# Latent attention of a two-block kernel: rotation on transposed features, softmax by groups of heads, first tile against its own keys

## The reference, cut to what matters

```python
def mla_mixer(x, cos, sin, w_in, q_norm, kv_norm, w_uq, w_ukv, w_out):
    c_q, c_kv, k_rope = jnp.split(x @ w_in, [256, 512], axis=-1)        # 256 + 256 + 64 columns
    q  = (rms_norm(c_q, q_norm) @ w_uq)    # 8 heads x (128 plain + 64 rotated)
    kv = (rms_norm(c_kv, kv_norm) @ w_ukv) # 8 heads x (128 key + 128 value)
    q_rope = rope(q_rope, cos, sin); k_rope = rope(k_rope, cos, sin)   # one rotated key for all heads
    s  = (q_nope . k_nope + q_rope . k_rope) * 192 ** -0.5
    s  = where(key_chunk <= query_chunk, s, -inf)    # chunks of 64 tokens
    return (softmax(s) @ v) @ w_out                  # w_out: 1024 x 1024
```

## Time and profile before

| | us |
|---|---|
| median of three runs | 3115.67 |
| profiled execution | 3120.56 |
| its span, first to last instruction | 3118.6 |
| PE busy | 2941.4 (94%) |
| DVE busy | 1938.2 (62%) |
| ACT busy | 1544.7 (50%) |
| mean granted TensorE clock | 0.966 of full |

### The profile page before, as it was taken

How to read it: one execution, slowest core, us unless ns; L and a number is a source line. 1 busy time by engine, 2 the same in 40 slices (tenths; PEclk the granted TensorE clock), 3 DMA queues, 4 the chain that set the end, 5 groups by cost and what they waited for, 6 DMA issues and landing times.

```text
span 3118.6 us, 38381 instructions
## 1 busy us (share of the span) xinstructions
PE 2941.4 (94%) x15294; PEld 2454.3 (79%) x15294; DVE 1938.2 (62%) x2879; ACT 1544.7 (50%) x2264; POOL 73.5 (2%) x98
## 2 busy tenths in 40 slices
PE   8999999899999999998999999985999999999999
PEld 6879878678788798776788878873788878887887
DVE  5556977665565579775655764562545764567645
ACT  5554734455455546434554644452444544464554
POOL 0000000000000000000000000000000000000000
PEclk9999998899999999998999999996999999999999
DMA  7544410355555434104554445540454655452552
GB/s 280 186 141 152 155 48 15 125 185 186 172 192 186 163 129 136 42 8 162 185 186 167 154 158 182 169 166 27 145 182 152 212 181 186 163 191 96 191 182 81
DMA packets 127650, 469.40 MB, mean 151 GB/s; under 512 B 14478, under 2 KB 14654, under 8 KB 126320
## 3 DMA queue, kind: packets, MB, share of 16 engines
q1 hardware_dynamic: 124416, 452.55, 42.6%
q0 software_dynamic: 3056, 14.39, 1.4%
HBM read 465.84 MB, written 1.05 MB: 150 GB/s over the span
## 4 chain that ended last, share of the span: by engine, by line
PE 79%; DVE 12%; ACT 5%; issue 2%; POOL 1%; DMA 0%; POOLq 0%; ACTq 0%; DVEq 0%
PE ps L589 76%; DVE w_lo_part L1920 2%; PE ps L761 2%; DVE hc L2226 1%; DVE conv_acc L2151 1%; ACT w_hi_part L1399 1%; PE ps L626 1%; ACT wx_hi_part L1399 0%; DVE wx_lo_part L1920 0%; DVE h_lo_part L1962 0%; DVE x_res L2063 0%; DVE zs L2369 0%; ACT gdn_rhs L1666 0%; POOL gdn_gate L2671 0%; DVE x_res L2121 0%
## 5 line engine op out<-in xcount | busy, mean ns | idle before, releaser
L1920 DVE TENSOR_TENSOR w_lo_part<-w_raw,w_hi_part 128x1024 fp32r<-128x1024 f32 x458 | 551.2, 1216 | 366.4 <-ACT w_hi_part L1399 365.0
L1399 ACT ACTIVATE w_hi_part<-w_raw 128x1024 fp32r<-128x1024 f32 x458 | 476.3, 1053 | 421.4 <-PE ps L589 421.3
L589 PE MATMUL ps<-w_hi_part,h_hi_part 128*128 128x512 f32 (+2 forms) x1348 | 543.2, 403 | 35.9 <-DVE w_lo_part L1917 8.6
L589 PE MATMUL ps<-w_hi_part,h_lo_part 128*128 128x512 f32 (+2 forms) x1348 | 529.6, 393 | 0.0
L589 PE MATMUL ps<-w_lo_part,h_hi_part 128*128 128x512 f32 (+2 forms) x1348 | 529.5, 393 | 0.0
L1920 DVE TENSOR_TENSOR wx_lo_part<-wx_raw,wx_hi_part 128x1024 fp32r<-128x1024 f32 x222 | 268.2, 1220 | 218.2 <-ACT wx_hi_part L1399 217.8
L1399 ACT ACTIVATE wx_hi_part<-wx_raw 128x1024 fp32r<-128x1024 f32 x222 | 231.6, 1057 | 231.4 <-PE ps L589 231.3
L589 PEld LDWEIGHTS ps<-w_hi_part,h_hi_part 128*128 128x128 f32 x1348 | 259.7, 193 | 96.6 <-issue 18.3
L589 PEld LDWEIGHTS ps<-w_hi_part,h_lo_part 128*128 128x128 f32 x1348 | 259.2, 192 | 55.2
L589 PEld LDWEIGHTS ps<-w_lo_part,h_hi_part 128*128 128x128 f32 x1348 | 260.1, 193 | 49.8
L589 PE MATMUL ps<-wx_hi_part,h_hi_part 128*128 128x512 f32 x712 | 285.7, 401 | 6.4 <-ACT lv L1729 2.1
(11 more groups left out here) (432 smaller groups left out, 4857.9 us busy)
## 6 DMA issues: line engine op xcount, KB each, us to landing
w_raw<-in_weights SPq DMA_DIRECT2D x568, 512.0 KB, 3.3
wx_raw<-in_weights SPq DMA_DIRECT2D x288, 512.0 KB, 3.3
row<-in_rows POOLq DMA_DIRECT2D x8, 1024.0 KB, 5.2
row<-in_rows POOLq DMA_DIRECT2D x8, 512.0 KB, 4.0
const<-in_const SPq DMA_DIRECT2D x1, 1088.0 KB, 16.1
x_res<-in_x SPq DMA_DIRECT2D x2, 512.0 KB, 6.5
ple_p<-in_p POOLq DMA_DIRECT2D x4, 256.0 KB, 5.1
out<-x_res SPq DMA_DIRECT2D x2, 512.0 KB, 2.6
```

Of the source, the lines that this page charges most:

```text
L589: return nc.tensor.matmul(out, lhsT, rhs_, start=start, stop=stop, skip_group_check=True)
L1399: A(hi_of(s)[:, 0:wd], raw_of(s)[:, 0:wd], ACT.Copy).then_inc(*up("w_hi", u))
L1920: V.tensor_tensor(lo_of(s)[:, 0:wd], raw_of(s)[:, 0:wd], hi[:, 0:wd], ALU.subtract).then_inc(*up("w_lo", u))
```

## The change

Only `mla` and what feeds it is changed, on all engines.

- **Head.** The norm weights are no longer columns applied after the turn but a row (`mnorm`) applied before it. Each tile has its own square root and its own turn (`turn_c`). The angles are computed with features on partitions and the 256 tokens in the free dimension.
- **Rotation.** The packing adds the rotated-query weights with the halves of each head exchanged (`mla_uq_swap`) and the rotated-key weights beside their exchanged copy (`mla_kr`). The rotation becomes product times cosine plus exchanged product times signed sine, on features, with no turn afterwards. For the key the sum is taken by PE with the identity. There is one more weight unit (857 instead of 856), and the key's unit is full width.
- **Softmax.** Heads are scored in groups: for tile 0 two groups of four heads against 128 keys, for tile 1 four groups of two heads against 256 keys. The mask is a third matmul into the last 64 keys with one contraction row (`mrow`, `mla_masked` in the trace). Maxima and exponentials read PSUM; DVE, no longer ACT, copies the turned probabilities. PE's order interleaves the groups.
- **Output.** The last product takes its input tile by tile and half by half, as the gated linear attention did.

Of `mla`'s own functions the diff shows the new lines; the lines that they replace stand in the listing above.

```diff
-            rows("mla_w_in_2", j, 0, 512, MR)
-            for c in range(0, MH, 4):
-                feature("mla_uq_nope", j, c * P, 2, 4)
-            rows("mla_uq_rope", j, 0, 0, 512)
-            for c in range(0, MH, 4):
-                feature("mla_uk", j, c * P, 2, 4)
+            feature("mla_kr", j, 0)
+            feature("mla_uq_rope", j, 0, 2, 4)
+            feature("mla_uq_swap", j, 0, 2, 4)
+            for w in ("mla_uq_nope", "mla_uk"):
+                for c in range(0, MH, 4):
+                    feature(w, j, c * P, 2, 4)
...
+        HEADS = [[[0, 2, 4, 6], [1, 3, 5, 7]], [[0, 2], [1, 3], [4, 6], [5, 7]]]
+        SCORE_BANK = [[2, 3], [6, 7, 4, 5]]
...
+                def turn_c(t):
                     pe.wait_ge(*when("mcn", (tag, t)))
                     for c in range(4):
+                        last_ = nc.tensor.transpose(ps[:, t, c * P:(c + 1) * P], mcn[:, t, c * P:(c + 1) * P], ident)
+                    last_.then_inc(*up("turned", (tag + ".c", t)))
+
+                def chunks(banks, first, key):
+                    s = next_unit()
+                    for c in range(4):
+                        out = ps[:, banks[c // 2], (c % 2) * SEQ:(c % 2 + 1) * SEQ]
+                        last_ = feature_chunk(s, out, mc_hi[:, first:first + 2], mc_lo[:, first:first + 2], 2, c * 2)
+                    last_.then_inc(*up("w_used", key))
+
+                def score(t, g):
+                    tok, nk = slice(t * P, (t + 1) * P), (t + 1) * P
+                    for n, h in enumerate(HEADS[t][g]):
+                        o = ps[:, SCORE_BANK[t][g], n * nk:(n + 1) * nk]
+                        b = (h % 2) * MR
+                        mm(o, mqnT[:, h, tok], mknT[:, h, 0:nk], True, False)
+                        mm(o, mqrT[b:b + MR, h // 2, tok], mkrT[b:b + MR, 0:nk], False, False)
+                        last_ = mm(o[:, nk - CH:], mrow[0:1, 0:P], mrow[0:1, P:], False, True)
+                    last_.then_inc(*up("mscore", (tag, t, g)))
+
+                def turn_p(t, g):
+                    pe.wait_ge(*when("mexp", (tag, t, g)))
+                    if t and g >= 2:
+                        pe.wait_ge(*when("mpT_out", (tag, t, g - 2)))
+                    elif t:
+                        pe.wait_ge(*when("mpT_out", (tag, 0, g)))
+                    for n, h in enumerate(HEADS[t][g]):
+                        for k in range(t + 1):
+                            at = (n * (t + 1) + k) * P
+                            last_ = nc.tensor.transpose(ps[:, g % 2, at:at + P], msc[t][:, slot_of(h), k * P:(k + 1) * P], ident)
+                    last_.then_inc(*up("mpT", (tag, t, g)))
+
+                def output(t, b):
+                    pe.wait_ge(*when("mpT_out", (tag, t, 2 * b + 1 if t else 1)))
+                    for h in range(4 * b, 4 * b + 4):
+                        for k in range(t + 1):
+                            last_ = mm(ps[:, (6 if t else 2) + b, (h % 4) * P:(h % 4 + 1) * P], mpT[t][:, slot_of(h), k, :],
+                                       mv[:, k, h * P:(h + 1) * P], k == 0, k == t)
+                    last_.then_inc(*up("mo", (tag, t, b)))
+
+                turn_c(0)
+                s = next_unit()
+                feature_chunk(s, ps[:, 6, 0:SEQ], h_hi, h_lo, KC).then_inc(*up("w_used", ("mkr", tag)))
+                turn_c(1)
+                pe.wait_ge(*when("mkr_parts", tag))
+                for n in range(2):
+                    o = ps[n * MR:(n + 1) * MR, 3, 0:SEQ]
+                    mm(o, ident[:, 0:MR], mkr[:, :], True, False)
+                    last_ = mm(o, ident[:, MR:], mkr[:, :], False, True)
+                last_.then_inc(*up("mkr_sum", tag))
+                for t in range(NT):
+                    pe.wait_ge(*when("h_lo", (tag + ".c", t)))
+                chunks([6, 7], 0, ("mqr", (tag, 0)))
+                chunks([0, 1], 0, ("mqr", (tag, 1)))
                 pe.wait_ge(*when("mkr_out", tag))
+                chunks([2, 3], 0, ("mqn", (tag, 0)))
+                chunks([4, 5], 0, ("mqn", (tag, 1)))
+                pe.wait_ge(*when("roped", (tag, 0)))
+                chunks([6, 7], 2, ("mkn", (tag, 0)))
+                pe.wait_ge(*when("roped", (tag, 1)))
+                chunks([0, 1], 2, ("mkn", (tag, 1)))
+                slots = [next_unit(), next_unit()]
+                for t in range(NT):
+                    pe.wait_ge(*when("mT", (tag, "q", t)))
+                    for k in range(2):
+                        last_ = row_chunk(slots[k], lambda t, n: ps[:, 2 + 2 * t + n, :], mc_hi[:, 2 + k, :], mc_lo[:, 2 + k, :],
+                                          0, k == 0, k == 1, tiles=[t])
+                        if t:
+                            last_.then_inc(*up("w_used", *([("product", tag + ".v")] if k else [])))
+                    if t == 0:
+                        last_.then_inc(*up("mv_first", tag))
+
+                pe.wait_ge(*when("roped", (tag, 2)))
+                pe.wait_ge(*when("mT", (tag, "k", 1)))
+                pe.wait_ge(*when("mrow", tag))
+                pe.wait_ge(*when("evacuated", (tag + ".v", 0)))
+                score(0, 0)
+                score(0, 1)
+                score(1, 0)
+                turn_p(0, 0)
+                score(1, 1)
+                turn_p(0, 1)
                 pe.wait_ge(*when("evacuated", (tag + ".v", 1)))
+                score(1, 2)
+                output(0, 0)
+                output(0, 1)
+                score(1, 3)
+                turn_p(1, 0)
+                turn_p(1, 1)
+                output(1, 0)
+                turn_p(1, 2)
+                turn_p(1, 3)
+                output(1, 1)
...
+                def exps(t, g):
+                    nk = (t + 1) * P
+                    act.wait_ge(*when("mmax", (tag, t, g)))
+                    for n, h in enumerate(HEADS[t][g]):
+                        p = slot_of(h)
+                        A(msc[t][:, p, :], ps[:, SCORE_BANK[t][g], n * nk:(n + 1) * nk], ACT.Exp, scale=MLA_SCALE,
+                          bias=mst[:, 1, t, p:p + 1], accum_out=mst[:, 2, t, p:p + 1]).then_inc(*up("mexp", (tag, t, g)))
+
+                square(0)
                 act.wait_ge(*when("angle", tag))
+                A(rope[:, :, :], red[:, :, :], ACT.Sin).then_inc(*up("sine", tag))
+                take_c(0)
+                square(1)
+                weights(4)
+                take_c(1)
                 weights(1)
+                act.wait_ge(*when("mkr_sum", tag))
+                A(mkrT[:, :], ps[:, 3, 0:SEQ], ACT.Copy).then_inc(*up("mkr_out", tag))
                 weights(2)
+                copied(mqnT, 2, "q", 0)
+                weights(1)
+                copied(mqnT, 4, "q", 1)
+                weights(1)
+                copied(mknT, 6, "k", 0)
+                weights(1)
+                copied(mknT, 0, "k", 1)
+                weights(1)
+                act.wait_ge(*when("mv_first", tag))
+                A(mv[:, 0, :], acc(2, 0), ACT.Copy).then_inc(*up("evacuated", (tag + ".v", 0)))
                 act.wait_ge(*when("w_used", ("product", tag + ".v")))
+                A(mv[:, 1, :], acc(2, 1), ACT.Copy).then_inc(*up("evacuated", (tag + ".v", 1)))
+                exps(0, 0)
+                exps(0, 1)
+                for g in range(4):
+                    exps(1, g)
+                weights(2)
...
                 dve.wait_ge(*when("mla_in", tag))
+                link(V.tensor_copy(angle[:, :], posi[:, :]))
+                link(V.tensor_scalar(angle[:, :], angle[:, :], invf[:, 0:1], None, ALU.mult))
                 for n, shift in enumerate((0.0, 0.25)):
+                    link(V.tensor_scalar(turns[:, n, :], angle[:, :], 1.0 / TWO_PI, shift, ALU.mult, ALU.add))
+                link(V.tensor_scalar(turns[:, :, :], turns[:, :, :], ROUND, None, ALU.add))
+                link(V.tensor_scalar(turns[:, :, :], turns[:, :, :], ROUND, None, ALU.subtract))
+                link(V.scalar_tensor_tensor(red[:, :, :], turns[:, :, :], -PI_PARTS[0], over(angle[:, :], 2), ALU.mult, ALU.add))
+                for part in PI_PARTS[1:]:
+                    link(V.scalar_tensor_tensor(red[:, :, :], turns[:, :, :], -part, red[:, :, :], ALU.mult, ALU.add))
+                link(V.tensor_scalar(red[:, 1, :], red[:, 1, :], 0.25 * TWO_PI, None, ALU.add))
+                V.tensor_scalar(red[:, :, :], red[:, :, :], PI_IN, -PI_IN, ALU.min, ALU.max).then_inc(*up("angle", tag))
+                link(V.memset(mrow[0:1, 0:P], 0.0))
+                link(V.memset(mrow[0:1, 0:CH], 1.0))
+                V.memset(mrow[0:1, P:], -1e30).then_inc(*up("mrow", tag))
+                mean(0)
+                normed_c(0)
+                take_c(0)
+                mean(1)
+                normed_c(1)
                 weights(4)
+                dve.wait_ge(*when("sine", tag))
+                dve.wait_ge(*when("w_used", ("mkr", tag)))
+                for n in range(2):
+                    r = slice(n * MR, (n + 1) * MR)
```

(36 more changed lines are left out.)

293 lines of the change are left out of this document (93 added, 200 removed).

## The result

The kernel after takes 3076.3 us (median of 4, 3074.6 to 3078.22), the kernel before 3119.69 in the runs beside it. The ratio is 0.9859 with a 95% interval of 0.9842 to 0.9876, so 39 to 49 us less, 44 in the middle. The forecast was 48 less, from 3115.67 to 3068. The measured 3076.3 is 8.3 above that figure and outside the 3062 to 3073 that the prediction gave 0.58, though inside its wider 3059 to 3082; 4.0 of it is that the kernel before took 3119.69 here and not 3115.67. Between the two profiled executions the spans differ by 42.2 us (3118.6 to 3076.4).

The account below looks back on a forecast made before the run. It took PE's stream of matmuls, 79% of the chain, as the bound. Head +4.9, projections +1.4, rotation -14.7 and attention -39.6 sum to -48.0 us, from 3115.67 to 3068; range 3062 to 3073 (0.58), wider 3059 to 3082.

Parts of the forecast that it names:

- Piece 3: Rotation, between projections and scores: small instructions, wait, turns and copies go, 14.7 us becomes 0.
- Piece 2: Projections, first up-projection to their end: 23.0 us becomes 24.4, 1.4 us more, half-clock start included.
- Piece 1: Head, latent product to first up-projection: starts 4.9 us later, bounds +2 to +9.
- four float32 matmuls of 256 columns, 1.15 us each: In the head, PE's adding of the rotated key's parts at half clock: 4.6 us.
- Piece 4: Attention, first score to first output matmul: 74.2 us becomes 34.6, 39.6 us less.
- A float32 matmul of 128 columns is 0.26, the mask 0.23.: Full-clock score prices in the attention, giving tile 0 6.0 us and PE's work there 27.0 us.
- Scores keep the clock.: In the attention, scores hold PEclk at 1.00 but don't raise it; 1.5 us added for drops at the end waits.
- the prediction's own sign: Stated test in the attention: the prediction is wrong if PEclk reads 0.50 during tile 1's scores.
- My first rival: Any gap in tile 1's scores drops PEclk to 0.50, costing 8.5 us: 3075; cases at 3074 to 3076 together 0.22.
- the head didn't become the bound: Rival: the head's serial chain takes its upper end and masks cost 0.4: 3075; cases at 3074 to 3076 together 0.22.
- Columns are saved: Rival denied: 128-column score matmuls cost as much as 256, tile 0 8 x 0.74 more: 3074; cases 3074 to 3076 together 0.22.
- The slow case: Rival: PE stays at half clock through attention, output projection and first MLP, 3119 us; not faster or slower 0.04.

Follow-up runs that it names:

- e10: Kernel before with rotary products contracting over 128 rows, using two zeroed key copies: 3104.6 us against 3120.51, ratio 0.9946.
- e2: Kernel after with the rotary product contracting over all 128 rows and the mask matmuls left out: 3050.86 us, ratio 0.9791 against the kernel before.
- e5: Kernel after with every score matmul, rotary and mask, zero-padded to 128 rows and nothing left out: 3054.92 us, ratio 0.9791 against the kernel before.
- e3: Kernel after with the 16 mask matmuls left out, all else unchanged: 3058.26 us, ratio 0.9815 against the kernel before.
- e6: Kernel after with only the mask matmul filled up to 128 rows; rotary product keeps 64: 3062.16 us, ratio 0.9817 against the kernel before.
- e7: Kernel after with only the rotary product filled up to 128 rows; mask keeps one row: 3060.48 us, ratio 0.9809 against the kernel before.
- e11: e7 with each one-row mask matmul issued three times: 3082.8 us, ratio 0.9876 against the kernel before.
- e4: Kernel after with the rotary key's product moved ahead of the first latent turn: 3075.46 us, ratio 0.9869 against the kernel before.

## Why the prediction came near, step by step

**Piece 3 was right.** PE goes from the values to the scores without a wait.

**Piece 2 was right**, 24.2 for 24.4, the slow start included.

**Piece 1 was right in its mechanism and mis-sized in one term.** Both waits stand where they were forecast. The term "four float32 matmuls of 256 columns, 1.15 us each" took 1.9 us for 4.6. Two things were wrong in it. The 1.15 came from the stretch whose row counts alternate; without that a matmul costs 0.85 at half clock (e10, 2121.99 to 2122.84). And the four fill two halves of the array's columns; their weight loads stand in pairs in the trace (2084.11, 2084.60, 2085.02), and they took about the time of two: 2 x 0.85 = 1.7. That is 2.7 of the 3.3 us; the rest, 0.6, are the angles. The root came as forecast.

**Piece 4 is the step that failed: "74.2 becomes 34.6".** Its order was right: the softmax is hidden, and the waits of 1.15, 1.78 and 0.97 us stand where they were forecast (1.3, 1.6, 1.3). Two prices were wrong.

- *"A float32 matmul of 128 columns is 0.26, the mask 0.23."* The row it came from the earlier trace rows is a stream in which all matmuls have 128 rows. In the scores each had another row count than its neighbour: 0.42 and 0.36. For the whole piece at full clock, tile 0 would take 8 x 1.19 = 9.5, tile 1 8 x 1.565 = 12.5 (the last group, 3.13 for two heads), turns 3.1, values 48 x 0.118 = 5.7: 30.8 instead of 27.0. With waits and the last turns the piece would be 35.7. So this error is 2.6 us of the 13.3. The 0.63 of 256 columns was right only because its row comes from such a mixed stream, pairs of 128 and 64 rows. The Trainium skill has a rule that would explain it (TensorEngine Tiling (Array Packing), "Key Properties"): changing the tiling mode, not just the tile, drains the engine. e2 and e5 agree, in that 0.20 us a matmul goes where the counts are equal; that a change from 128 rows to 64 or 1 is such a change of mode is my reading, which I had not applied, as I took 64 rows for a shorter product and not for another mode.
- *"Scores keep the clock."* 47.9 - 35.7 = 12.2 us went to half clock, where 1.5 stood in the sum. By the prediction's own sign it was wrong here: PEclk reads 0.50 in three of tile 1's four groups. My first rival, the clock lost in tile 1's scores, gave the loss 8.5 us, but it had neither the place nor the trigger. The clock fell in tile 0's scores, and the trigger was to be a gap, of which there was none. The prediction looked only at whether PE was busy; e3, e6, e7 and e11 show that what it is busy with counts as well. The rule of the Trainium skill that the prediction weighed (TensorE: Matmul & The Clock Gate, "A second HAM failure mode: psum-queue depth-cycling") has the right effect, a clock that falls, by another mechanism: it wants idling between the groups, and this trace has none.

The rivals: the head didn't become the bound of the total (17.3 us for its 20.6). The softmax is hidden. Columns are saved: a pair costs 0.83 at 128 columns and 1.26 at 256, though by 0.42 a pair and not by the 0.74 I had. The slow case needed the half clock to last into the output projection, where PEclk is 1.00.

That the saving of 44 us came within 4 of the forecast owes something to luck: the attention missed by 13.3 us, and 7.7 came back from the head (3.3), the projections (0.2) and the unchanged code before and behind the stage (4.2, for which no cause is shown).

## What to carry to other kernels

Price a matmul from a row whose neighbours have the same number of contraction rows; where a stream mixes 128, 64 and 1 rows, add about 0.2 us for each matmul whose count differs from its neighbours', or pad with zero rows, which cost PE no time of their own here (e2, e5). PE being busy is not enough to keep its clock: here PE ran 27 us at half of it without a wait, most of them scores of 128, 64 and 1 rows. So read PEclk under every stretch that mixes row counts. When a wait is filled with other work and little is gained, as in e4 (0.5 us), read what the releasing engine had in front of that item, and move that.
